# FoX key tiles in groups of two, first loads in two parts, and the causal mask as a GpSimd selection

## The chip, the cores and the metric

One core of a Trainium2 chip runs the whole program. The metric is the time of one execution on the device in microseconds (us), the median of several runs. The engines are TensorE (PE in the rows; PEld is its weight load), VectorE (DVE), ScalarE (ACT), GpSimd (POOL) and SyncE (SP), which issues nearly all transfers.

## The reference

A transformer block with two gated attention branches, in float32. For the change the FoX branch matters, causal attention with a forget gate:

```python
u = rmsnorm(h, g_pre);  q, k, v, z, f, gates = split(u @ w_in)
# FoX branch, 8 heads of 64, 1040 tokens (16 learned ones ahead of 1024)
logits = (q @ k.T) * 64**-0.5 + (c[t] - c[s])          # c = cumsum(log_sigmoid(f))
logits = where(s <= t, logits, -1e30)                  # the causal mask
y_fox = softmax(logits) @ v * silu(z_fox)
# SWA branch: a band of 128 tokens and the 16 learned ones, ALiBi, a sink in the softmax
m = sigmoid(g_swa) * (y_swa @ w_up_swa) + sigmoid(g_fox) * (y_fox @ w_up_fox)
out = h + rmsnorm(m @ w_out)
```

## The kernel before

The program has four stages, one behind the other on TensorE: RMSNorm, transposes and the plain projections; products for the other projections (query, gate, z), which end at 495 us; **attention**, 505 to 678 us; up-projection, merge and output. This case is about attention.

**FoX** runs over 4 pairs of heads (j), 2 halves of the queries (q, 512 columns each) and the key tiles of 128 (i: 5 for the first half, 9 for the second): 14 **units** a pair, 56 in all, numbered u. The function `key_tile` gives a unit's width, 512 columns, or 512, 400, 272, 144 and 16 where the diagonal cuts it; ten of fourteen units are cut by the diagonal and masked. For each unit TensorE does the step **tile** (key times query into PSUM, two float32r matmuls for each head, L1964 and L1965, and for a masked unit a bfloat16 matmul more, L1970, that adds -1e30 over up to 128 columns). ScalarE takes the exponential into the ring `p_fox` (L1352). The step **values** then multiplies it by V (L1984, four matmul records of 64 output rows), and GpSimd and VectorE add the exponentials up in `acc` (L1194, L1199 and L1749). When a half is complete, **den** sums `acc` over the keys on TensorE (L1994), ScalarE copies it to `den_row` (L1378), VectorE takes four reciprocals (**rec**, L1755) and multiplies (**fin**, L1762 and L1765).

**SWA** is spread between the units as 32 **items**: **score** on TensorE (L1944, L1945), maximum on VectorE (L1703 to L1711), exponential on ScalarE (L1364), reciprocal (`rec`, L1721) on VectorE and **norm** on GpSimd (L1175), transposes **trans** on TensorE (L2003), copied to `p_t` by ScalarE (even items) or VectorE (odd ones, L1727), **pv_swa** on TensorE (L2017) and the product with z into `y` on VectorE (L1734). There is one PSUM bank for pv_swa's result, so it waits for the y of the item before (`swa_y`).

`attention_steps` writes one list of steps. Every engine walks this list and issues its own part of each step, in that order and no other; semaphores hold the data together. An engine that waits in one step holds up all its later steps. In the list of before, unit u's tile is followed by a norm and a score, the values of unit u-1, an exponential, a den or rec, one pv_swa and one trans. The queries, keys and values of pair 0 are loaded by SyncE during the last couple of products, and behind them the values of SWA (`v_a`, `v_b`), for which the first score waits (`swa_loaded`).

Of the kernel before, what the change touches and what calls it, by code (L numbers as in the profile page):

```python
# [60 lines left out]
PT_RING = 6  # L61
PSWA_RING = 2
PROB_RING = 3
# [159 lines left out]
def attention_steps():  # L223
# [3 lines left out]
    def score(i):  # L227
        return item("score", i)
# [10 lines left out]
    spread = len(units) - 8  # L239
    next_item, unnormed, normed, untransposed, unvalued = 0, None, None, None, None  # L240
    closing = []
    for u, (j, q, i) in enumerate(units):
        first, last = i == 0, i == 4 * q + 4
        x = u % per
        steps.append(dict(kind="tile", j=j, q=q, i=i, u=u, first=first, last=last))
        if j + 1 < PAIRS:
            for turn, what in ((1, "load_queries"), (2, "load_z"), (3, "load_keys"), (5, "load_values")):
                if x == turn:
                    steps.append(dict(kind=what, j=j + 1, u=u))
        if (j, x) in ((0, 7), (0, 9)):  # L250
            steps.append(dict(kind="load_up", d=(x - 7) // 2, u=u))
        untransposed, normed = normed, unnormed
        if unnormed is not None:
            steps.append(item("norm", unnormed))
            unnormed = None
        slot = next_item < ITEMS and (u + 1) * ITEMS // spread > u * ITEMS // spread
        if slot:
            steps.append(score(next_item))
        if u:
            pj, pq, pi = units[u - 1]  # L260
            steps.append(dict(kind="values", j=pj, q=pq, i=pi, u=u - 1, first=pi == 0, last=pi == 4 * pq + 4))
        if slot:
            steps.append(item("exp", next_item))
            unnormed = next_item
            next_item += 1
        if closing and closing[0][0] <= u:
            steps += closing.pop(0)[1]
        if unvalued is not None:
            steps.append(item("pv_swa", unvalued))
            unvalued = None  # L270
        if untransposed is not None:
            steps.append(trans(untransposed))
            unvalued = untransposed
        if last:
            closing.append((u + 2, [dict(kind="den", j=j, q=q)]))
            closing.append((u + 3, [dict(kind="rec", j=j, q=q, c=c) for c in range(2)]))
            closing.append((u + 4, [dict(kind="rec", j=j, q=q, c=c) for c in (2, 3)] + [dict(kind="fin", j=j, q=q)]))
        if j == PAIRS - 1:
            turn = {1: 0, 3: 1, 5: 2, 7: PAIRS + 2, 9: PAIRS - 1, 10: PAIRS, 11: PAIRS + 1}
            if x in turn:  # L280
                steps.append(dict(kind="split_y", s=turn[x], c0=0, c1=2))
            if x == 12:
                steps.append(dict(kind="split_y", s=2 * PAIRS - 1, c0=0, c1=1))
            if x == 4:
                steps.append(dict(kind="split_up", d=0))
            if x == 8:
                steps.append(dict(kind="split_up", d=1))
    j, q, i = units[-1]
    steps.append(dict(kind="values", j=j, q=q, i=i, u=len(units) - 1, first=False, last=True))
    for _, extra in closing:  # L290
        steps += extra
    steps.append(dict(kind="split_y", s=2 * PAIRS - 1, c0=1, c1=2))
    assert next_item == ITEMS and unvalued is None and unnormed is None and untransposed is None and normed is None

    uses, count, splits = [], {"dve": 0, "act": 0}, 0
    for st in steps:
# [1815 lines left out]
```

## Time and profile before

| | us |
|---|---|
| median of 3 runs (lowest, highest) | 869.65 (867.27, 871.06) |
| the profiled execution's own time | 866.6 |
| its span | 864.8 |
| attention, first FoX matmul to first matmul of the up-projection | 505 to 678 |
| GpSimd busy from 505 to 678 | 103.8 |
| VectorE busy from 505 to 678 | 117.8 |

The span is the profiled execution from its first to its last instruction. In a row of a timeline the first number is the start in the span, the second the length, then engine, line, operation, output and inputs; in brackets stands the idle time before it and what ended that. A matmul's length is modelled and overlaps the next one's; the distance between two starts is what it takes.

### The profile page before, as it was taken

What the parts mean: (1) busy time and instruction counts of PE and PEld (TensorE: products, weight loads), DVE (VectorE), ACT (ScalarE), POOL (GpSimd) and SP (SyncE); (2) the same over time, 40 slices, a digit from 0 to 9 for tenths busy, and PEclk for the clock granted to TensorE, in tenths of its full rate; (3) what the DMA queues carried; (4) which work ended last, traced back from release to release, by engine and by line L of the source; (5) the groups of instructions that cost most, each with busy time, mean ns of one, the idle gap of its engine ahead of it and who ended that gap; (6) DMA issues with size and microseconds to landing.
All of it is one profiled execution on the core that took longest, in us unless ns stands there. A gap on an engine that the chain in (4) does not pass through costs nothing.

```text
span 864.8 us, 12858 instructions
## 1 busy us (share of the span) xinstructions
PE 809.0 (94%) x4514; PEld 651.2 (75%) x4514; DVE 500.1 (58%) x1050; ACT 314.6 (36%) x637; POOL 348.1 (40%) x284
## 2 busy tenths in 40 slices
PE   3999989999999999999999959998988799999996
PEld 3999989887878878878878746656654578878885
DVE  7934886357677686565564627676777434442112
ACT  6431241333333323333333236565667022232111
POOL 3412322444445444434444025655557244412221
PEclk9999999999999999999999979999999799999999
DMA  9331424569964626636635799946500645533221
GB/s 285 106 116 51 124 68 129 124 171 261 242 176 145 171 86 185 172 98 181 158 113 130 185 233 247 256 124 172 124 1 2 212 131 147 143 127 125 97 91 73
DMA packets 120879, 124.99 MB, mean 145 GB/s; under 512 B 29824, under 2 KB 91344, under 8 KB 120816
## 3 DMA queue, kind: packets, MB, share of 16 engines
q1 hardware_dynamic: 119376, 119.92, 50.9%
q10 hardware_dynamic: 1440, 4.26, 1.3%
q8 instruction: 36, 0.59, 0.3%
q14 instruction: 27, 0.22, 0.1%
HBM read 90.93 MB, written 34.92 MB: 146 GB/s over the span
## 4 chain that ended last, share of the span: by engine, by line
PE 76%; DVE 9%; issue 4%; SPq 3%; DMA 3%; POOL 2%; ACT 2%; DVEq 0%; ACTq 0%; POOLq 0%
PE PS L1827 18%; PE PS L1828 18%; PE PS L1829 18%; PE PS L2063 3%; PE PS L2065 3%; PE PS L2064 3%; PE PS L1924 2%; PE PS L1984 2%; DVE t_val L1579 2%; PE PS L1964 1%; SPq L871 1%; PE PS L1965 1%; PE PS L2003 1%; DMA QBs<-q_dram 1%; POOL acc L1199 1%
## 5 line engine op out<-in xcount | busy, mean ns | idle before, releaser
L1130 POOL TENSOR_TENSOR ops<-s_sum,ops 128x512 fp32r<-128x512 f32 x64 | 87.4, 1376 | 114.1 <-ACT ops L1228 114.1
L1827 PE MATMUL PS<-t_hi,ops 128*128 128x512 f32 x256 | 101.1, 395 | 0.0
L1828 PE MATMUL PS<-t_lo,ops 128*128 128x512 f32 x256 | 99.8, 390 | 0.0
L1829 PE MATMUL PS<-t_hi,ops 128*128 128x512 f32 x256 | 99.8, 390 | 0.0
L1130 POOL TENSOR_TENSOR ops<-raw,ops 128x512 fp32r<-128x512 f32 x48 | 65.0, 1354 | 70.0 <-ACT ops L1228 69.9
L1199 POOL TENSOR_TENSOR acc<-acc,p_fox 128x400 f32<-128x400 f32 (+5 forms) x76 | 61.5, 830 | 2.5 <-ACT p_fox L1352 0.9
L1151 POOL TENSOR_TENSOR w_plain<-raw,w_plain 128x1024 fp32r<-128x1024 f32 x10 | 28.0, 2801 | 85.0 <-ACT w_plain L1257 85.0
L1658 DVE TENSOR_TENSOR z_tmp<-u,PS 128x512 f32<-128x512 f32 x48 | 33.0, 687 | 48.9 <-PE PS L1829 28.1
L1352 ACT ACTIVATE p_fox<-PS,neg_c_col 128x512 f32<-128x512 f32 (+5 forms) x112 | 54.1, 532 | 17.2 <-PE PS L1970 14.4
L1228 ACT ACTIVATE ops<-s_sum 128x512 fp32r<-128x512 f32 x64 | 39.6, 624 | 54.9 <-DVE s_sum L1460 41.1
L1829 PEld LDWEIGHTS PS<-t_hi,ops 128*128 128x128 f32 x256 | 48.1, 188 | 10.6
L1827 PEld LDWEIGHTS PS<-t_hi,ops 128*128 128x128 f32 x256 | 48.3, 188 | 9.3
L1828 PEld LDWEIGHTS PS<-t_lo,ops 128*128 128x128 f32 x256 | 48.1, 188 | 8.9
L1964 PE MATMUL PS<-QA,KA 128*128 128x512 f32 (+5 forms) x112 | 42.9, 391 | 12.6 <-DMA KB<-k_dram 9.8
L1329 ACT ACTIVATE stage_b<-z_tmp,half_bg 128x512 f32<-128x512 f32 x32 | 23.2, 724 | 85.4 <-DVE z_tmp L1658 85.4
L1827 PE MATMUL PS<-y_hi,up_hi 128*128 128x512 f32 x128 | 51.0, 398 | 2.4 <-POOL up_lo L1136 1.4
L1175 POOL TENSOR_TENSOR probs<-probs,rec 128x416 f32<-128x416 f32 x32 | 29.6, 924 | 53.5 <-DVE rec L1721 53.5
L1827 PE MATMUL PS<-uA_hi,ops 128*128 128x512 f32 x128 | 50.9, 397 | 0.0
L1828 PE MATMUL PS<-uA_lo,ops 128*128 128x512 f32 x128 | 50.8, 397 | 0.0
L1828 PE MATMUL PS<-y_lo,up_hi 128*128 128x512 f32 x128 | 50.8, 397 | 0.0
L1829 PE MATMUL PS<-y_hi,up_lo 128*128 128x512 f32 x128 | 50.7, 396 | 0.0
L1829 PE MATMUL PS<-uA_hi,ops 128*128 128x512 f32 x128 | 50.3, 393 | 0.0
(203 smaller groups left out, 2192.1 us busy)
## 6 DMA issues: line engine op xcount, KB each, us to landing
raw<-in_w_in_dram SPq DMA_DIRECT2D x34, 512.0 KB, 5.2
q_dram<-stage_b SPq DMA_DIRECT2D x32, 256.0 KB, 3.0
g_dram<-stage_b SPq DMA_DIRECT2D x32, 256.0 KB, 2.0
tanh_g<-g_dram SPq DMA_DIRECT2D x16, 512.0 KB, 3.9
max_k<-k_dram SPq DMA_DIRECT2D x16, 260.0 KB, 5.3
max_c<-neg_c_dram SPq DMA_DIRECT2D x8, 520.0 KB, 6.0
KA<-k_dram SPq DMA_DIRECT2D x8, 520.0 KB
x_all<-in_x_dram SPq DMA_DIRECT2D x8, 512.0 KB, 8.1
```

Source lines behind the costliest of these rows:

```text
L1130: nc.gpsimd.tensor_tensor(ops[:, i % OPS, 1], op_source(p, name), ops[:, i % OPS, 0].bitcast(F32), ALU.subtract).then_inc(op_ready, 1)
L1151: nc.gpsimd.tensor_tensor(w_plain[:, t, 1], raw[:, s], w_plain[:, t, 0].bitcast(F32), ALU.subtract).then_inc(w_ready, 1)
L1175: nc.gpsimd.tensor_tensor(probs[:, b, :, 0:W_SWA], probs[:, b, :, 0:W_SWA], scale, ALU.mult).then_inc(swa_normed, 1)
L1199: nc.gpsimd.tensor_tensor(dst, other, tile, ALU.add).then_inc(acc_done["pool"], 1)
L1228: nc.scalar.activation(ops[:, i % OPS, 0], op_source(p, name), ACT.Copy).then_inc(op_hi_ready, 1)
L1352: nc.scalar.activation(p_fox[0:keys, n % PT_RING, 0:w], PS[0:keys, S_BANKS[n % S_RING], 0:w], ACT.Exp, bias=neg_c_col[0:keys, i, 2 * j + h ...
L1658: nc.vector.tensor_tensor(src, partial, product(p, "S1" if name == "S3" else name), ALU.add).then_inc(folded, 1)
L1827: pe.matmul(dst, hi_w, hi, start=first, stop=False)
L1828: pe.matmul(dst, hi_w, lo, start=False, stop=False)
L1829: return pe.matmul(dst, lo_w, hi, start=False, stop=last)
L1964: pe.matmul(dst, KA[n][:, h, kk], QA[n][:, h, tok], start=True, stop=False)
L2063: pe.matmul(dst, m_hi[:, k, tok], hi, start=k == 0, stop=False)
```

## The change

Four edits. (1) The list of steps goes by **groups** of two units, numbered g from 0 to 28: both tiles, the norms of the group before, one or two scores (a group with g divisible by 3 with rest 2 has two, up to g = 23), both values of the group before, exponentials, den with the first two reciprocals or the last two with fin, then all pv_swa of items scored two groups ago and all trans of items scored one group ago. (2) The causal mask leaves TensorE. GpSimd writes zeros over the masked part of the exponentials, two instructions for each of the 40 masked units, in the step values ahead of the additions, and the values matmul waits for them (`fox_masked`). (3) The first tiles of pair 0 wait for a first part of the loads alone (5 of 9 key tiles, half of the queries, 5 value tiles); the second parts are issued ahead of `v_a` and `v_b`, twelve transfers more in that place, and are waited for at unit 5. (4) `p_fox` has 8 buffers for 6, the ring `probs` 4 for 3.

```diff
-PT_RING = 6
+PT_RING = 8
-PROB_RING = 3
+PROB_RING = 4
@@ attention_steps: the list of steps, one group of two units at a time
-    spread = len(units) - 8
-    for u, (j, q, i) in enumerate(units):
-        steps.append(dict(kind="tile", j=j, q=q, i=i, u=u, first=first, last=last))
...
+    groups = len(units) // 2
+    spread = groups - 4
+    for g in range(groups + 1):
+        now = range(2 * g, 2 * g + 2) if g < groups else ()
+        for u in now:
+            steps.append(dict(kind="tile", j=j, q=q, i=i, u=u, first=i == 0, last=i == 4 * q + 4))
...
+        for n in scored:
+            steps.append(item("norm", n))
+        turned, scored = scored, []
+        if g < spread:
+            scored = list(range(g * ITEMS // spread, (g + 1) * ITEMS // spread))
+        for n in scored:
+            steps.append(score(n))
+        for u in range(2 * g - 2, 2 * g) if g else ():
+            j, q, i = units[u]
+            steps.append(dict(kind="values", j=j, q=q, i=i, u=u, first=i == 0, last=i == 4 * q + 4))
+        for n in scored:
+            steps.append(item("exp", n))
+        due = [x for x in closing if x[0] <= g]
+        closing = [x for x in closing if x[0] > g]
+        for _, extra in due:
+            steps += extra
+        for n in transposed:
+            steps.append(item("pv_swa", n))
+        for n in turned:
+            steps.append(trans(n))
+        transposed = turned
+        for u in now:
+            if i == 4 * q + 4 and g < groups - 1:
+                closing.append((g + 2, [den, rec 0, rec 1]))
+                closing.append((g + 3, [rec 2, rec 3, fin]))
...
@@ SyncE, in the last couple of the products
-                        load_values(sp, 0)
+                        load_values(sp, 0, fox_first, 0, 5)
-                        load_queries_fox(sp, 0)
+                        load_queries_fox(sp, 0, fox_first, 0, 4)
-                        load_keys_fox(sp, 0)
+                        load_keys_fox(sp, 0, fox_first, 0, 5 * P)
+                        load_keys_fox(sp, 0, fox_loaded[0], 5 * P, LENGTH)
+                        load_queries_fox(sp, 0, fox_loaded[0], 4, NQ)
+                        load_values(sp, 0, fox_loaded[0], 5, NK)
                         sp.dma_start(v_a[0:A_ROWS, 0, :], vd[0, 0:A_ROWS]).then_inc(swa_loaded, 16)
@@ GpSimd, at the step "values"
+                    for h in range(2):
+                        n = 2 * u + h
+                        if n in mask_of:
+                            tile = p_fox[n % PT_RING][0:keys, 0:masked]
+                            pool.wait_ge(fox_exp, n + 1)
+                            nc.gpsimd.affine_select(tile, tile, [[1, masked]], ALU.is_ge, 0.0, base=shift,
+                                                    channel_multiplier=-1).then_inc(fox_masked, 1)
@@ TensorE, at the step "tile"
-                    if i == 0 and q == 0:
+                    if (j, q, i) == (0, 0, 0):
+                        pe.wait_ge(fox_first, 16 * FIRST_LOADS)
+                        pe.wait_ge(halves_cleared, 3)
+                    elif i == 0 and q == (0 if j else 1):
                         pe.wait_ge(fox_loaded[j], 16 * FOX_LOADS)
-                    if masked:
-                        for h in range(2):
-                            pe.matmul(PS[0:keys, S_BANKS[(2 * u + h) % S_RING], 0:masked], causal[:, 0:keys],
-                                      ident_b[:, shift:shift + masked], start=False, stop=True).then_inc(tile_done, 1)
@@ TensorE, at the step "values"
                         pe.wait_ge(fox_exp, x + 1)
+                        if x in mask_of:
+                            pe.wait_ge(fox_masked, mask_of[x])
```

In the diff "den", "rec" and "fin" in the closing lists are written short. The order that comes out of it, first for **VectorE** around the den of pair 0's second half (group 8; `den_row` is rec of FoX, `rec<-den` is the reciprocal for a norm of SWA). Before:

```order
L1755 RECIPROCAL den_row<-den_row 128x128 x2
L1734 SCALAR_TENSOR_TENSOR y<-PS,y 128x128
L1727 COPY p_t<-PS 128x512
L1721 RECIPROCAL rec<-den 128x2
L1703 TENSOR_SCALAR far_alibi<-const 128x16
```

and with the change:

```order
L1786 RECIPROCAL den_row<-den_row 128x128 x2
L1763 SCALAR_TENSOR_TENSOR y<-PS,y 128x128
L1756 COPY p_t<-PS 128x512
L1750 RECIPROCAL rec<-den 128x2 x2
L1732 TENSOR_SCALAR far_alibi<-const 128x16
```

The order of kinds is the same; behind the two den reciprocals now stand two norm reciprocals, and the den itself stands in the same group's steps instead of one unit earlier.

**GpSimd** right behind that place, at group 9, whose values are those of units 16 and 17 (272 and 144 columns). Before:

```order
L1175 TENSOR_TENSOR probs<-probs,rec 128x2x208
L1199 TENSOR_TENSOR acc<-acc,p_fox 128x272 x2
L1175 TENSOR_TENSOR probs<-probs,rec 128x2x208
L1199 TENSOR_TENSOR acc<-acc,p_fox 128x144 x2
```

with the change:

```order
L1195 TENSOR_TENSOR probs<-probs,rec 128x2x208 x2
L1209 AFFINE_SELECT p_fox<-p_fox 128x128 x2
L1228 TENSOR_TENSOR acc<-acc,p_fox 128x272 x2
L1209 AFFINE_SELECT p_fox<-p_fox 128x128 x2
L1228 TENSOR_TENSOR acc<-acc,p_fox 128x144 x2
```

The selections stand behind two norms, and the second unit's behind the first unit's additions.

**TensorE** at units 7 and 8. Before, from the tile of unit 8 to one pv_swa:

```order
L1964 MATMUL PS<-QA,KA 128x512
L1965 MATMUL PS<-QB,KB 128x512
L1964 MATMUL PS<-QA,KA 128x512
L1965 MATMUL PS<-QB,KB 128x512
L1944 MATMUL PS<-kk_s,QAs 128x208
L1945 MATMUL PS<-kk_s,QBs 128x208
L1944 MATMUL PS<-kk_s,QAs 128x208
L1945 MATMUL PS<-kk_s,QBs 128x208
L1984 MATMUL PS<-p_fox,VF 64x512 x2
L2017 MATMUL PS<-p_t,v_a 64x128 x2
L2017 MATMUL PS<-p_t,v_b 64x128 x2
```

with the change, in group 4, behind the tiles of units 8 and 9 and a score:

```order
L2015 MATMUL PS<-p_fox,VF 64x512 x4
L2025 MATMUL PS<-acc,ones 64x512 x2
L2048 MATMUL PS<-p_t,v_a 64x128 x2
L2048 MATMUL PS<-p_t,v_b 64x128 x2
L2048 MATMUL PS<-p_t,v_a 64x128 x2
L2048 MATMUL PS<-p_t,v_b 64x128 x2
L2034 MATMUL PS<-ident,probs 80x128 x2
```

The values of two units (6 and 7) stand together, a den has come into the same group, and two pv_swa stand back to back.

## Rows read from the trace of the kernel before

**Rows 1.** Page, part 1: busy us, share of the span and instructions of each engine.
```profile
PE 809.0 (94%) x4514; PEld 651.2 (75%) x4514; DVE 500.1 (58%) x1050; ACT 314.6 (36%) x637; POOL 348.1 (40%) x284
```

**Rows 2.** Busy time in stretches of attention: PE, PEld, DVE, ACT, POOL, clock, DMA.
```profile
505.00:678.00 173.00, 154.68 (x1072) 98.25 (x1072) 117.75 (x339) 104.50 (x274) 103.81 (x122) 0.93 0.57 139
502.00:504.00 2.00, 0.00 (x0) 0.00 (x0) 0.00 (x0) 0.00 (x0) 0.00 (x0) 0.50 1.05 197
...
545.00:600.00 55.00, 52.21 (x386) 34.66 (x384) 37.43 (x120) 33.94 (x96) 32.18 (x42) 0.94 0.68 168
630.00:655.00 25.00, 20.54 (x132) 12.72 (x131) 16.87 (x45) 15.71 (x39) 15.69 (x19) 0.86 0.00 1
```

**Rows 3.** Waits of PE, 500 to 680: total, times, longest.
```profile
PE PS L1964 <- DMA KB<-k_dram: 9.8, 1, 9.8
PE PS L2017 <- DVE p_t L1727: 4.8, 3, 2.1
PE PS L1994 <- POOL acc L1199: 4.3, 2, 3.5
PE PS L1944 <- DVE neg_max L1711: 3.5, 2, 3.1
PE PS L1964 <- ACT p_fox L1352: 2.8, 5, 1.2
```

**Rows 4.** Timeline of PE in pair 1.
```profile
566.61 0.40 PE L1965 MATMUL PS<-QB,KB 128*128 128x512 f32 x1
566.94 1.08 PE L1984 MATMUL PS<-p_fox,VF 128*64 128x512 f32 x4
567.95 0.63 PE L2003 MATMUL PS<-ident,probs 128*80 128x128 f32 x4
...
569.11 0.39 PE L1965 MATMUL PS<-QB,KB 128*128 128x512 f32 x1
569.34 0.26 PE L1944 MATMUL PS<-kk_s,QAs 128*128 128x208 f32 x1
...
569.86 1.08 PE L1984 MATMUL PS<-p_fox,VF 128*64 128x512 f32 x4
570.77 0.39 PE L2017 MATMUL PS<-p_t,v_a 80*64 80x128 f32 x4
...
572.47 0.40 PE L1965 MATMUL PS<-QB,KB 128*128 128x512 f32 x1
...
572.80 0.34 PE L1944 MATMUL PS<-kk_s,QAs 128*128 128x208 f32 x1
...
573.41 1.08 PE L1984 MATMUL PS<-p_fox,VF 128*64 128x512 f32 x4
```

**Rows 5.** Groups by line and shape, 494 to 679: busy us, mean ns.
```profile
L1175 POOL TENSOR_TENSOR probs<-probs,rec 128x416 f32<-128x416 f32 x32 | 29.6, 924 | 53.5 <-DVE rec L1721 53.5
...
L1199 POOL TENSOR_TENSOR acc<-acc,p_fox 128x272 f32<-128x272 f32 x16 | 13.3, 852 | 0.0
...
L1199 POOL TENSOR_TENSOR acc<-acc,p_fox 128x144 f32<-128x144 f32 x16 | 8.0, 517 | 0.0
...
L1199 POOL TENSOR_TENSOR acc<-acc,p_fox 16x16 f32<-16x16 f32 x8 | 1.6, 211 | 0.0
```

**Rows 6.** Timeline of VectorE behind a den.
```profile
526.99 1.76 DVE L1755 RECIPROCAL den_row<-den_row 128x128 f32<-128x128 f32 x2
...
528.81 0.68 DVE L1727 COPY p_t<-PS 128x512 f32<-128x512 f32 x1
```

**Rows 7.** Timeline of SyncE's queue: last transfer before the first score.
```profile
494.92 0.62 SPq L1061 DMA_DIRECT2D v_b<-v_dram  x1
```

**Rows 8.** Transfers issued 478 to 520: KB each, median us to landing.
```profile
v_b<-v_dram SPq DMA_DIRECT2D x1, 512.0 KB, 13.1
```

**Rows 9.** Timeline of POOL at the end of attention.
```profile
663.01 5.37 POOL L1199 TENSOR_TENSOR acc<-acc,p_fox 128x512 f32<-128x512 f32 x3
669.07 5.98 POOL L1199 TENSOR_TENSOR acc<-acc,p_fox 128x400 f32<-128x400 f32 x7 [0.69 <-DVE acc L1749]
```

More of the change, by code:

```diff
@@ L238, in attention_steps @@
     per = len(units) // PAIRS
-    spread = len(units) - 8
-    next_item, unnormed, normed, untransposed, unvalued = 0, None, None, None, None
+    groups = len(units) // 2
+    spread = groups - 4
+    scored, transposed = [], []
     closing = []
-    for u, (j, q, i) in enumerate(units):
-        first, last = i == 0, i == 4 * q + 4
-        x = u % per
-        steps.append(dict(kind="tile", j=j, q=q, i=i, u=u, first=first, last=last))
[L246 to L287, printed above, removed]
@@ L288, in attention_steps @@
     j, q, i = units[-1]
-    steps.append(dict(kind="values", j=j, q=q, i=i, u=len(units) - 1, first=False, last=True))
-    for _, extra in closing:
-        steps += extra
+    steps += [dict(kind="den", j=j, q=q)] + [dict(kind="rec", j=j, q=q, c=c) for c in range(4)]
+    steps.append(dict(kind="fin", j=j, q=q))
     steps.append(dict(kind="split_y", s=2 * PAIRS - 1, c0=1, c1=2))
-    assert next_item == ITEMS and unvalued is None and unnormed is None and untransposed is None and normed is None
+    assert not closing and not scored and not transposed
@@ L442, in build @@
         VF[1] = sb("VF1", [P, NK, P], on=ph2)
-        p_fox = sb("p_fox", [P, PT_RING, BANK], on=ph2)
+        p_fox = [sb(f"p_fox{n}", [P, BANK], on=ph2) for n in range(6)]
         sb("gap", [P, 64], on=ph2)
@@ L843, in natural, with load_queries_fox @@
             return PS[:, 2 * (n % 4):2 * (n % 4) + 2, :].rearrange("p a b -> p (a b)")
-        def load_queries_fox(queue, j):
-            n, done = j % 2, fox_loaded[j]
-            q_hi, q_lo = (qd[PAIRS + j, x] for x in range(2))
+        def load_queries_fox(queue, j, done, t0, t1):
+            n, cols = j % 2, slice(P * t0, P * t1)
+            q_hi, q_lo = (qd[PAIRS + j, x][:, cols] for x in range(2))
             for half in (Q0, Q1):
-                queue.dma_start(QA[n][half].bitcast(F32),
+                queue.dma_start(QA[n][half, :, cols].bitcast(F32),
@@ L858, in load_keys_fox @@
-        def load_keys_fox(queue, j):
-            n, done = j % 2, fox_loaded[j]
-            k_hi, k_lo = (kd[1 + j, x] for x in range(2))
+                queue.dma_start(QB[n][row:row + 1, h, cols].bitcast(F32),
+                                max_dram[2 * j + h, t0:t1].rearrange("(o t) q -> o (t q)", o=1)).then_inc(done, 16)
+        def load_keys_fox(queue, j, done, c0, c1):
+            n, cols = j % 2, slice(c0, c1)
+            k_hi, k_lo = (kd[1 + j, x][:, cols] for x in range(2))
             for half, src in ((Q0, k_hi), (Q1, k_lo)):
-                queue.dma_start(KA[n][half].bitcast(F32),
+                queue.dma_start(KA[n][half, :, cols].bitcast(F32),
@@ L1189, in _ @@
                             continue
+                        if n in mask_of:
+                            pool.wait_ge(fox_masked, mask_of[n])
                         dst = acc[0:keys, f % 2, h, c0:c0 + w]
-                        tile = p_fox[0:keys, n % PT_RING, 0:w]
+                        tile = p_fox[n % PT_RING][0:keys, 0:w]
                         pool.wait_ge(fox_exp, n + 1)
```

77 lines of the change are left out of this document (56 added, 21 removed).

## The prediction

> **What bounds the kernel now.** The page's busy shares come first: TensorE is busy for 94% of the span, all others for 58% or less [rows 1]. Busy matmuls are modelled, so what counts is where TensorE waits, and the change touches attention alone. The stretches show 154.7 us of matmuls in the 173 us from 505 to 678, with VectorE at 117.8 and GpSimd at 103.8, at a mean clock of 0.93 [rows 2]. Behind this stands the table of TensorE's waits: 9.8 us for pair 0's keys, 4.8 for `p_t` from VectorE, 3.5 for a score's bank from VectorE, 2.8 for exponentials, and 4.3 for `acc` from GpSimd, of which 3.5 is one wait at the end [rows 3]. So TensorE bounds attention with little slack, and where it waits, VectorE or GpSimd is behind.
>
> **The change part by part. Matmuls of the mask.** 40 pairs go. With a mask the score starts 0.33 us after the last tile matmul (572.47 to 572.80), without 0.23 (569.11 to 569.34); and a score behind a mask takes 0.61 us to the values (572.80 to 573.41) against 0.52 (569.34 to 569.86) [rows 4]. That is 0.19 us for a mask ahead of a score (24 of them by the order) and 0.10 for the others (16): 4.6 + 1.6 = 6.2 us less.
>
> **Fewer changes of kind.** A values matmul behind a tile starts after 0.33 us (566.61 to 566.94), a matmul of the tile's own kind after 0.23; four values matmuls take 0.91 us to a pv_swa (569.86 to 570.77), which has the same 64 rows, and 1.01 to a trans (566.94 to 567.95) [rows 4]. So each change between the kinds costs 0.10 us. Counted in the order there are 141 in attention before and 77 now: 64 x 0.10 = 6.4 us less.
>
> **Waits that go.** If the new list were only denser, TensorE's waits in the middle would be other ones: I take out all of 4.8 + 3.5 + 2.8 + 0.8 = 11.9 us [rows 3], and the time at the lower clock, 6% of 55 us and 14% of 25 us [rows 2], 3.3 + 3.5 = 6.8 us. Together with the matmuls that is 31.3 us less. These are the credits.
>
> **The price of a selection.** The trace has no such instruction. Its nearest rows on GpSimd: 0.21 us for a sum of 16 x 16, 0.52 for a two-input sum of 144 columns [rows 5]. A selection over up to 128 columns with one input lies between; I take 0.30 us, 0.6 for a unit's two, 24 us in all on an engine that has 103.8 busy of 173 [rows 2]. That leaves room for the sum of work but not for the place: GpSimd does it behind the norms, ahead of which TensorE now waits.
> On GpSimd's elementwise work the Trainium skill ("GPSIMD Engine Reference", Elementwise side-by-side cycle accounting) gives about 2 cycles an element for a compare and select that is not unrolled and 2.6 for two inputs. An estimate from that page is 128 x 2.03 / 1.2 GHz = 0.22 us for a selection, and the row of 0.52 us for 144 columns is above its two-input figure (0.31), by a fixed part; with 0.22 the waits below would shrink by some 2 us.
>
> **The new chain of waits.** In before, GpSimd's norm is needed by a trans alone, and TensorE waited little for it. Now values wait for a selection, which waits behind the norms, which wait for VectorE's reciprocal, which in VectorE's order stands behind the den reciprocals, y and `p_t`. Two places show the size.
> *Group 9*, 0 being TensorE's start of group 8. Tiles of 272 and 144 columns, two scores, values of 512 and 400, den: matmuls until 4.6. ScalarE copies `den_row` until 5.3. VectorE then needs 1.8 us to `p_t` and 0.6 for that [rows 6]: 7.8. Only now come the two reciprocals and on GpSimd two norms of 0.88 [rows 5], until 9.6, and the first selection, 9.9. TensorE began group 9 at 5.6 and wanted it at 7.5: 2.4 us of waiting. The second unit's selection stands behind two sums of 272 columns, 0.73 each when they overlap (1.45 for two, [rows 5] gives 0.85 singly), and comes at 12.0, 1.5 us after TensorE is ready. Group 9 loses 3.9 us; groups 16 and 23, with one norm, 3.0 each.
> *Group 12* lies behind the den of the first half: the same chain, and two norms and a sum of 512 columns ahead of unit 23's selection: 3.1 us. Groups 5 and 19 have one norm, 2.3 each; group 26 has none left.
> *Groups 6, 13, 20* follow a group in which VectorE had rec, rec and fin behind a late sum; their norm starts some 2.7 us after TensorE wants the selection behind it, and two selections are waited for: 4.6 each, 5.4 in group 6 with two norms.
> Sum: 9.9 + 7.7 + 14.6 = 32.2 us.
>
> **Two pv_swa in one group** (8 groups). The second waits for the y of the first, which takes 0.2 us and a semaphore each way; I take 0.5 us: 4.0. In three of them (4, 22, 25) VectorE does two den reciprocals of 0.88 first [rows 6]: 1.6 more each, 4.8. Sum 8.8.
>
> **The end.** The last exponential sums run on GpSimd without a gap for 11.4 us [rows 9] and then release the den (the wait of 3.5 us [rows 3]). Ten selections come into this stretch: 3.0 us, and 1 us for a split that ScalarE now issues behind a den: 4.0.
>
> **The first loads.** They buy nothing. With half of the queries, three eighths of the keys and four ninths of the values no longer ahead (about 1.5 MB less at some 200 GB/s [rows 2]) TensorE starts pair 0 some 7 us earlier, does two tiles (2 us), and then the first score waits for `v_b`, as before. That transfer was issued at 494.92 and landed 13.1 us later, at 508.0 [rows 7, 8], with the DMA engines at 1.05 of their time [rows 2]: the bytes ahead of it are the same, and twelve more transfers, 0.6 us of issue each as the row of `v_b` has it [rows 7], put it at 502.6 on the queue. So it lands at 508 at the earliest, up to 510. Before, the score began at 508.9. And TensorE, idle again until then, starts at the lower level of its clock (granted 0.50 of 2.4 GHz in that stretch [rows 2]) with the whole list ahead instead of two tiles: 2.0 us more. From both sides: 1 us less to 4 us more.
> The Trainium skill speaks against this part ("DMA: Bandwidth & Descriptors", Rules for kernel authors): it advises few transfers of 1 MiB or more. By the trace the queue is full in any case; by the page the smaller pieces would also move fewer bytes a microsecond, which would put `v_b` later still, no earlier.
>
> **Sum.** 32.2 + 8.8 + 4.0 + 2.0 = 47.0 us more, 31.3 less: 15.7 more. Against the profiled execution's own 866.6 that gives 882.3; that execution lies 3.05 us below the median of 869.65, so the same difference on the median gives 885.4. I say 884.
>
> **The rivals.**
> *Faster, the list is dense and the chain is hidden* (0.29). VectorE and GpSimd had 32% and 40% of attention free [rows 2]. If VectorE reaches the norm's reciprocal two microseconds earlier than I reckon (the den's group starts late enough, or ScalarE's copy comes earlier), then the 32.2 us shrink to some 8, and the waits for pv_swa stay: 866.6 - 31.3 + 8 + 8.8 + 6 = 858, on the median 861; with the pv_swa waits at 0.5 us, 856. It decides from half of the mask waits on: below 16 us the change gains. For it speaks that TensorE waited for a norm hardly at all before; against it that VectorE's order puts four things ahead.
> *No change* (0.13): the mask waits come out at 13 to 20 us, 866 to 874.
> *Slower by much, GpSimd becomes the bound* (0.16). At 0.52 us a selection, the upper bound, GpSimd has 103.8 + 42 = 146 us to do in attention, in order, and idles wherever VectorE is late; each wait above grows by 0.4 to 0.9 us and the end by 2.2: 12 to 20 us more, 895 to 905.
> *My forecast* (0.42): 876 to 893.
> That the mask would not leave TensorE is excluded by the order.
>
> **How the numbers follow.** A measurement of this kernel tells 0.5% (4.3 us) from no change. Slower: 0.42 + 0.16 = 0.58; the same 0.13; faster 0.29. Since both signs hold much of the chance, the range must reach into the faster case: 854 leaves out about 0.12 below, 904 about 0.06 above. The likeliest case alone has 876 to 893.
>
> **What would show it.** Right: among TensorE's waits a new group, values (L2015) for GpSimd's selection (L1209), 20 to 40 us in some 15 times, the longest just behind a den; GpSimd idle for VectorE's `rec`; pv_swa waiting for `y`; the first score waiting 6 to 8 us for `v_b` with two tiles ahead of it; attention's end 12 to 20 us later. No L1970, and 64 steps of 0.1 us fewer, so TensorE's own busy time in attention down by about 10 us. Wrong: the selections come ahead of need, their waits sum to less than 16 us, or a selection takes over 0.4 us; the first score starts before 507.

## The result: 6.6% slower, against a forecast of 1.7%

| | us |
|---|---|
| changed kernel, median of 4 runs (lowest, highest) | 927.57 (926.54, 928.58) |
| kernel before, 4 runs beside it | 870.36 (867.27, 872.48) |
| ratio, 95% interval | 1.066 (1.0625 to 1.0696) |
| span of the profiled execution, after and before | 926.2 and 864.8 |
| first matmul of the up-projection, after and before | 739.7 and 678.1 |

The 61.4 us by which the spans differ lie in attention: the products end at 495 us in both, and the up-projection starts 61.6 us later. (The medians differ by 57.2 us; the profiled execution of the kernel before, 866.6 us, was 3.8 below the median beside it. What follows compares the two profiled executions.) The stretch from 495 to that matmul, first of the kernel before and then of the changed one (length, then busy time of PE, PEld, DVE, ACT and POOL, the granted clock, the DMA share and GB/s):

```profile
495.00:678.00 183.00, 154.85 (x1073) 98.35 (x1072) 118.44 (x341) 105.94 (x276) 103.81 (x122) 0.92 0.59 143
```

```profile
495.00:739.70 244.70, 174.60 (x995) 119.39 (x993) 120.74 (x341) 108.22 (x276) 119.09 (x202) 0.82 0.46 107
```

By the page of the profile TensorE is busy for 90% of the span ([rows 1] has 94):

```profile
PE 830.4 (90%) x4434; PEld 674.1 (73%) x4434; DVE 502.0 (54%) x1050; ACT 316.8 (34%) x637; POOL 363.5 (39%) x364
```

In the stretch TensorE has 78 records fewer and is busy for 19.8 us more; the clock fell from 0.92 to 0.82. It is idle for 42 us more (70.1 for 28.2). So work and waits both grew, and the forecast had only the waits: it expected less work.

The waits of TensorE in the changed kernel from 495 to 745, the counterpart of [rows 3]:

```profile
PE PS L2015 <- POOL p_fox L1209: 36.0, 22, 5.2
PE PS L2048 <- DVE y L1763: 14.2, 8, 3.7
PE PS L1998 <- ACT p_fox L1381: 8.3, 12, 2.0
PE PS L1975 <- DMA v_b<-v_dram: 6.9, 1, 6.9
PE PS L1998 <- DMA KB<-k_dram: 2.7, 1, 2.7
```

The first is the new wait, values for the selection; the second is a group's second pv_swa, waiting for y of the first. How the longest of the first kind arises is seen in three timelines of group 6. VectorE:

```profile
546.51 1.76 DVE L1786 RECIPROCAL den_row<-den_row 128x128 f32<-128x128 f32 x2
548.30 0.69 DVE L1793 SCALAR_TENSOR_TENSOR den_row<-den_row,y 128x512 f32<-128x512 f32 x1
549.03 0.69 DVE L1796 TENSOR_TENSOR y<-PS,den_row 128x512 f32<-128x512 f32 x1
549.64 0.28 DVE L1763 SCALAR_TENSOR_TENSOR y<-PS,y 128x128 f32<-128x128 f32 x1
549.84 0.68 DVE L1756 COPY p_t<-PS 128x512 f32<-128x512 f32 x1
550.43 0.22 DVE L1750 RECIPROCAL rec<-den 128x2 f32<-128x2 f32 x2
```

GpSimd, in brackets its idle time and what ended it:

```profile
550.67 1.71 POOL L1195 TENSOR_TENSOR probs<-probs,rec 128x416 f32<-128x416 f32 x2 [7.31 <-DVE rec L1750]
552.33 0.54 POOL L1209 TENSOR_SCALAR_AFFINE_SELECT p_fox<-p_fox 128x128 f32<-128x128 f32 x2
552.84 2.01 POOL L1228 TENSOR_TENSOR acc<-acc,p_fox 128x400 f32<-128x400 f32 x2
554.80 0.54 POOL L1209 TENSOR_SCALAR_AFFINE_SELECT p_fox<-p_fox 128x128 f32<-128x128 f32 x2
```

and TensorE:

```profile
552.77 1.81 PE L2015 MATMUL PS<-p_fox,VF 128*64 128x400 f32 x4 [5.23 <-POOL p_fox L1209]
555.24 1.39 PE L2015 MATMUL PS<-p_fox,VF 128*64 128x272 f32 x4 [0.66 <-POOL p_fox L1209]
```

The two reciprocals that the norms need take 0.22 us, and stand behind 3.9 us of closing work. ScalarE had finished the exponentials of these units at 542.6 (four from 540.53 on, 2.06 us), and GpSimd has been idle for 7.3 us, so it could have made the selections long before; in its order they stand behind the norms. So an engine with half of its time free holds up the one that is the bound.

What such a wait does afterwards is seen in group 9. Stretches of the changed kernel: the wait, what follows it, and the next 7 us.

```profile
573.20:576.80 3.60, 0.18 (x3) 0.06 (x1) 3.56 (x13) 1.55 (x5) 2.13 (x4) 0.98 1.05 316
576.80:583.00 6.20, 5.20 (x25) 3.90 (x26) 2.44 (x5) 0.60 (x1) 3.35 (x7) 0.50 1.03 220
583.00:590.00 7.00, 6.45 (x46) 4.50 (x44) 2.30 (x11) 4.47 (x10) 2.55 (x7) 0.96 0.74 157
```

After 3.4 us of idle time TensorE works for 6.2 us at 0.50, which is the lower of its two levels, 1.2 GHz.

### The profile page after: what moved, and what is told of

Its sections match the earlier page's. It is cut to its first block, busy times and chain, and to the rows that moved or that the text cites. A ratio compares the mean times of both kernels' runs of the same rounds, so it can differ in the third digit from the quotient of the medians.

```text
span 926.2 us, 12871 instructions
## 1 busy us (share of the span) xinstructions
PE 830.4 (90%) x4434; PEld 674.1 (73%) x4434; DVE 502.0 (54%) x1050; ACT 316.8 (34%) x637; POOL 363.5 (39%) x364
## 4 chain that ended last, share of the span: by engine, by line
PE 63%; issue 11%; POOL 6%; DVE 6%; ACT 2%; DVEq 0%; ACTq 0%; POOLq 0%; DMA 0%
PE PS L1858 14%; PE PS L1859 14%; PE PS L1860 14%; PE PS L2094 3%; PE PS L2095 3%; PE PS L2096 3%; POOL acc L1228 2%; PE PS L1955 2%; PE PS L2015 2%; POOL probs L1195 1%; PE PS L2048 1%; PE PS L2034 1%; POOL p_fox L1209 1%; PE PS L1998 1%; PE PS L1999 1%
## 5 line engine op out<-in xcount | busy, mean ns | idle before, releaser
L2015 PE MATMUL PS<-p_fox,VF 128*64 128x512 f32 (+5 forms) x224 | 56.0, 552 | 36.1 <-POOL p_fox L1209 36.0
L1195 POOL TENSOR_TENSOR probs<-probs,rec 128x416 f32<-128x416 f32 x32 | 28.2, 893 | 128.3 <-DVE rec L1750 124.5
L2015 PEld LDWEIGHTS PS<-p_fox,VF 128*64 128x64 f32 (+1 forms) x224 | 18.9, 154 | 57.1 <-issue 49.9
L1687 DVE TENSOR_TENSOR z_tmp<-u,PS 128x512 f32<-128x512 f32 x48 | 32.9, 686 | 48.9 <-PE PS L1860 28.2
L1228 POOL TENSOR_TENSOR acc<-acc,p_fox 128x400 f32<-128x400 f32 (+5 forms) x76 | 55.5, 747 | 0.6
L1998 PE MATMUL PS<-QA,KA 128*128 128x512 f32 (+5 forms) x112 | 45.3, 411 | 11.2 <-ACT p_fox L1381 8.3
L1858 PE MATMUL PS<-uA_hi,ops 128*128 128x512 f32 x128 | 50.8, 397 | 0.0
```

Of the source, the lines that this page charges most:

```text
L1195: nc.gpsimd.tensor_tensor(probs[:, b, :, 0:W_SWA], probs[:, b, :, 0:W_SWA], scale, ALU.mult).then_inc(swa_normed, 1)
L1228: nc.gpsimd.tensor_tensor(dst, other, tile, ALU.add).then_inc(acc_done["pool"], 1)
L1687: nc.vector.tensor_tensor(src, partial, product(p, "S1" if name == "S3" else name), ALU.add).then_inc(folded, 1)
L1858: pe.matmul(dst, hi_w, hi, start=first, stop=False)
L1998: pe.matmul(dst, KA[n][:, h, kk], QA[n][:, h, tok], start=True, stop=False)
L2015: ins = pe.matmul(PS[h * HEAD:(h + 1) * HEAD, Y_BANKS[f % 2], c0:c0 + w], VF[j % 2][0:keys, i, h * HEAD:(h + 1) * HEAD], p_fox[x % PT_RING ...
```

## The experiments

Fifteen kernels, each read against the kernel before in its own runs. Beside the times stand numbers of the profiled execution from 495 us on: the selection and y columns are TensorE's waits for each; "ends" is the first matmul of the up-projection.

| kernel | median us | ratio (95%) | ends | PE busy | clock | selection | y |
|---|---|---|---|---|---|---|---|
| changed | 927.57 | 1.066 (1.0625 to 1.0696) | 739.7 | 174.6 | 0.82 | 36.0 | 14.2 |
| loads_one_part | 928.22 | 1.0657 (1.0626 to 1.0688) | 739.7 | 177.9 | 0.80 | 32.0 | 14.2 |
| fill_waits | 914.76 | 1.0493 (1.0451 to 1.0535) | 725.4 | 183.8 | 0.94 | 20.4 | 5.6 |
| mask_only | 914.53 | 1.0494 (1.0469 to 1.0518) | 726.8 | 171.4 | 0.83 | 47.4 | 0 |
| rec_early | 904.47 | 1.0376 (1.0352 to 1.0399) | 715.1 | 162.2 | 0.85 | 13.5 | 24.2 |
| select_first | 897.65 | 1.0302 (1.0271 to 1.0333) | 709.8 | 158.8 | 0.87 | 9.0 | 18.7 |
| groups_pe_mask | 893.43 | 1.0253 (1.0228 to 1.0279) | 704.5 | 161.8 | 0.88 | none | 19.6 |
| select_first_den_last | 889.93 | 1.0208 (1.0172 to 1.0245) | 700.5 | 153.8 | 0.92 | 7.4 | 9.1 |
| mask_first | 889.72 | 1.0205 (1.0161 to 1.025) | 701.5 | 161.3 | 0.87 | 27.0 | 0 |
| all_three | 888.96 | 1.0195 (1.0157 to 1.0232) | 699.6 | 153.8 | 0.90 | 7.4 | 13.2 |
| groups_pe_mask_den_last | 888.57 | 1.0175 (1.0123 to 1.0227) | 700.2 | 162.5 | 0.89 | none | 7.7 |
| groups_pe_mask_all | 886.02 | 1.0157 (1.012 to 1.0195) | 697.8 | 161.5 | 0.90 | none | 7.5 |
| all_four | 884.44 | 1.0143 (1.0095 to 1.0192) | 696.2 | 154.1 | 0.91 | 6.6 | 9.7 |
| late_values | 874.67 | 1.0039 (1.0015 to 1.0063) | 689.2 | 155.5 | 0.90 | 7.4 | 0 |
| rings_only | 872.12 | 1.0004 (0.9984 to 1.0023) | 684.0 | 157.2 | 0.90 | none | 0.6 |
| no_mask_before | 868.26 | 0.9958 (0.9943 to 0.9973) | 680.1 | 151.3 | 0.91 | none | 0.7 |

### One part undone, or one alone

**groups_pe_mask**, the mask back on TensorE:

```diff
-                        pe.matmul(dst, KB[n][:, h, kk], QB[n][:, h, tok], start=False, stop=True
-                                  ).then_inc(tile_done, 1)
+                        ins = pe.matmul(dst, KB[n][:, h, kk], QB[n][:, h, tok], start=False, stop=not masked)
...
+                            pe.matmul(PS[0:keys, S_BANKS[(2 * u + h) % S_RING], 0:masked], causal[:, 0:keys],
+                                      ident_b[:, shift:shift + masked], start=False, stop=True).then_inc(tile_done, 1)
```

Expected: 

> The changed kernel with the causal mask back on TensorE as before (all matmuls of the mask, no selection); groups, rings and the first loads in two parts stay. Chain theory (values wait for a selection that stands behind the norms; these 36 us of waits also take TensorE to its lower clock): the waits of values for GpSimd go, waits for a norm at the transposes come back for at most 8 us, mean clock in attention above 0.90, 880 to 892 us. Rival, the groups themselves are at fault (two pv_swa, scores, den and tiles in bundles, each engine in lockstep): the waits only move to the transposes and pv_swa, clock stays below 0.87, 905 to 925 us.

893.4: the selection accounts for 34 of the 57 us, and the groups alone cost 22 (first loads and rings included, which cost nothing that can be told, see below). Neither theory had it whole: the time is 1.4 us above the chain theory's range and the clock 0.88. The waits here are for y (19.6 us), for exponentials (11.1 in 18 places, against 2.8 in [rows 3]) and for norms (2.6).

**mask_only**, the other half: the selection in the kernel before, in its step values.

Expected: 

> The kernel before with the mask as a GpSimd selection alone, in the step values behind the norm; no groups, no split loads, rings as before. Chain theory: one norm for each unit stands ahead of each selection and VectorE's reciprocal ahead of that, 10 to 25 us of waits for the selection appear and the clock falls to 0.88 or so: 875 to 895 us. Rival, the groups are at fault: the selection alone is hidden, 4 to 7 us of mask matmuls are saved, 862 to 867 us.

914.5, beyond the range of both. The table of waits and, below it, one place on GpSimd:

```profile
PE PS L1998 <- POOL p_fox L1195: 47.4, 27, 4.3
PE PS L1981 <- DMA KB<-k_dram: 9.7, 1, 9.7
PE PS L2031 <- DVE p_t L1742: 1.6, 1, 1.6
```

```profile
631.93 0.88 POOL L1181 TENSOR_TENSOR probs<-probs,rec 128x416 f32<-128x416 f32 x1 [4.28 <-DVE rec L1736]
632.76 0.54 POOL L1195 TENSOR_SCALAR_AFFINE_SELECT p_fox<-p_fox 128x128 f32<-128x128 f32 x2
```

The same chain as in group 6, without any group: reciprocal, norm, selection, values. By itself the mask costs 4.9%, the groups 2.5%; together 6.6%. That the two don't add up would fit one wait that serves both units of a group (27 waits in `mask_only`, 22 in the changed kernel); no run shows it by itself.

**loads_one_part**, pair 0's loads as before:

```diff
-                        load_keys_fox(sp, 0, fox_first, 0, 5 * P)
-                        load_keys_fox(sp, 0, fox_loaded[0], 5 * P, LENGTH)
-                        load_queries_fox(sp, 0, fox_loaded[0], 4, NQ)
-                        load_values(sp, 0, fox_loaded[0], 5, NK)
+                        load_keys_fox(sp, 0, fox_loaded[0], 0, LENGTH)
```

Expected: 

> The changed kernel with pair 0's first loads in one part as before. My reckoning of the split (2 us lost, bounds 1 gained to 4 lost): 922 to 928 us, and the mean clock of attention stays at 0.82. Rival, the early start and the second wait for v_b are a main cause: below 915 us.

928.2, the ratio within 0.0003 of the changed kernel's, each known to some 0.003: the split does nothing that can be told. Its rows in the changed kernel are those foreseen, two tiles early and then the wait for `v_b`:

```profile
497.98 0.59 PE L1998 MATMUL PS<-QA,KA 128*128 128x512 f32 x1 [2.67 <-DMA KB<-k_dram]
...
508.10 0.54 PE L1975 MATMUL PS<-kk_s,QAs 128*128 128x208 f32 x1 [6.91 <-DMA v_b<-v_dram]
```

**rings_only**, the kernel before with 8 buffers for `p_fox` and 4 for `probs`. Expected: 

> The kernel before with the larger rings alone (8 buffers of exponentials for 6, 4 of probs for 3); mask on TensorE, no groups, no split loads. If buffers were never what was waited for: 869 to 872 us. If they take away a part of the waits for exponentials and accumulations: 863 to 868 us.

1.0004 (0.9984 to 1.0023): no effect that can be told.

**no_mask_before**, the kernel before with no mask at all. Expected: 

> The kernel before with the causal mask left out altogether (no mask matmul and no selection; its FoX branch attends to later tokens too). It sizes what taking the mask off TensorE can bring at most. My term was 6.2 us for the matmuls (0.19 and 0.10 us each): 862 to 866 us. Rival, VectorE and GpSimd pace the attention stage and the matmuls lie in their shadow: 868 to 872 us.

868.3, 0.42% faster (0.27 to 0.57%), 3.6 us. The stretch from 495 shows the same 3.6 us less of busy time (151.27 for 154.85), though in these two profiled executions the stretch itself isn't shorter (185.1 us for 183.0):

```profile
495.00:680.09 185.09, 151.27 (x994) 97.07 (x993) 118.39 (x341) 105.86 (x276) 103.78 (x122) 0.91 0.61 141
```

So in the order of before 40 pairs of mask matmuls cost 0.09 us each, not the 0.155 of my term, and no way of masking elsewhere could have won more than these 3.6 us (2.4 to 5.0). Two things limit the reading of busy times. `rings_only` has the matmuls of the kernel before and is busy for 157.2 us in its profiled execution, 2.3 more, so single executions agree to 2 or 3 us. And in the order by groups the mask matmuls show more: `groups_pe_mask_all` is busy for 161.5 us, `all_four` without them for 154.1, at clocks of 0.90 and 0.91, while their times differ by only 1.6 us.

### The place of the selection

**select_first** puts a group's selections ahead of its norms:

```diff
@@ GpSimd
+                if kind == "tile" and st["u"] >= 2 and st["u"] % 2 == 0:
+                    select(st["u"] - 2)
+                    select(st["u"] - 1)
```

Expected: 

> The changed kernel with the selections of a group issued by GpSimd ahead of the group's norms instead of behind them; nothing else. Chain theory: the waits of values for the selection fall from 36 to below 12 us, the clock rises from 0.82 to 0.88 or more, 885 to 900 us. Rival, the groups are at fault: other waits (pv_swa for y, tiles for exponentials, transposes for norms) grow in their place, 912 to 925 us. Rival, GpSimd has too much to do: its order changes nothing, 920 to 930 us.

897.7: the waits for the selection fall from 36.0 to 9.0 us, and the time by 30. Not all of this is waits. TensorE's idle time in the stretch fell by 14 us in all, since others took the place of some: y rose to 18.7, exponentials to 11.1, so a part of the rival holds too. The other 16 us are useful work, the same matmuls, which went from 174.6 to 158.8 us at a clock of 0.87.

**rec_early** attacks the same chain from VectorE:

```diff
@@ VectorE
-                elif kind == "norm":
+                elif kind == "exp":
                     i, b = st["i"], st["i"] % PROB_RING
                     dve.wait_ge(swa_exp, 2 * (i + 1))
```

Expected: 

> The changed kernel with VectorE's reciprocal for a norm moved to the end of its own group's scores, ahead of the den reciprocals, y and p_t, instead of the start of the next group; GpSimd's order unchanged (selection behind the norm). Chain theory as in the prediction (the reciprocal at the end of VectorE's group holds up norm and selection): waits for the selection fall from 36 to below 20 us, 895 to 912 us. Rival, GpSimd's own order (norms of 0.88 us and sums ahead of the selection) holds it up: 920 to 930 us. Rival, VectorE now waits for ScalarE's exponentials and is late with the sums and y: 928 us or more.

904.5: 36.0 to 13.5 us, with GpSimd's order as it was. Both ends of the chain are thus shown. The second rival takes its share: at `rec` VectorE now waits for ScalarE's exponentials for 22.6 us (1.6 before), and the waits for y come to 24.2 us.

**mask_first** and **late_values** do it in the order of before, unit by unit; `late_values` also has the larger rings and the values one unit later:

```diff
-        if u:
-            pj, pq, pi = units[u - 1]
+        if u > 1:
+            pj, pq, pi = units[u - 2]
```

Expected of the first: 

> The kernel before with the mask as a GpSimd selection alone (no groups, no split loads), and this time each unit's selection stands in the step tile of the next unit, ahead of the norm. Chain theory (what costs is the place behind the norm and VectorE's reciprocal): the 47 us of waits that the same selection cost behind the norm fall below 12, clock in attention back above 0.90, 862 to 875 us. Rival, GpSimd has 24 us more to do in a strict order and the norms and sums come late instead: 885 to 905 us.

Expected of the second: 

> The order of the kernel before, unit by unit, with the larger rings and the mask as a GpSimd selection issued in the tile step of the next unit, and the values of a unit one unit later than before (two units behind its tile), so that the selection has a whole unit of slack. Chain theory (it is the slack between a selection and its values matmul that decides): hardly any wait for a selection, clock above 0.92, 861 to 870 us. Rival, GpSimd's 24 us more in strict order are too much whatever the slack: 878 to 890 us.

`mask_first` gives 889.7, which lies in the rival's range and not in the theory's. Its mechanism is neither of the two pure: 27.0 us of waits for the selection remain, and no norm is waited for. The selection now stands ahead of its own unit's norm, but still behind the norm and the sums of the step before, so the old chain goes on through them. GpSimd at one of these waits, which ends at 516.51 after 2.89 us:

```profile
513.27 0.88 POOL L1194 TENSOR_TENSOR probs<-probs,rec 128x416 f32<-128x416 f32 x1 [3.55 <-DVE rec L1744]
514.10 2.01 POOL L1222 TENSOR_TENSOR acc<-acc,p_fox 128x400 f32<-128x400 f32 x2
516.07 0.54 POOL L1183 TENSOR_SCALAR_AFFINE_SELECT p_fox<-p_fox 128x128 f32<-128x128 f32 x2
```

`late_values` gives 874.7, 4.7 us above the theory's range and 3 below the rival's. Its waits, in a profiled execution of 877.9 us (the ten lie between 871.8 and 879.3):

```profile
PE PS L1997 <- DMA KB<-k_dram: 9.7, 1, 9.7
PE PS L2014 <- POOL p_fox L1191: 7.4, 5, 4.1
PE PS L1977 <- DVE neg_max L1742: 6.6, 4, 2.2
PE PS L2047 <- DVE p_t L1758: 4.4, 3, 2.8
```

With the same 80 selections on GpSimd the loss shrinks from 4.9% to 0.4%. Slack between a selection and its values, not GpSimd's throughput, is what the mask lacks. What remains in `late_values` is no gain all the same: `no_mask_before`, which has the same matmuls in the order of before and no selections, is 6.4 us faster.

### What a wait costs afterwards

**fill_waits** leaves the changed kernel as it is and adds matmuls that nobody reads, in 13 places ahead of the values and in 4 groups ahead of the second pv_swa:

```diff
+            def fill(group, times):
+                x, n = min(4 * group + 1, 111), min(group // 7, 3) % 2
+                pe.wait_ge(fox_exp, x + 1)
+                for _ in range(times):
+                    pe.matmul(PS[:, S_BANKS[x % S_RING], :], KA[n][:, 0, 0:P], QA[n][:, 0, 0:BANK],
+                              start=True, stop=True)
...
+                if kind == "values" and st["u"] in FILL:
+                    fill(st["u"] // 2 + 1, FILL[st["u"]] * 3 // 4)
```

Expected: 

> The changed kernel with some 120 matmuls more that nothing reads (keys times queries of 512 columns into a free score bank, 0.23 us each at the upper level, some 28 us together), placed on TensorE ahead of the waits for the selection and for y that were longer than 1 us; they should fit into the waits. Clock theory (the waits also cost afterwards, since TensorE then works at 1.2 GHz for a while): with more matmuls the kernel gets faster, mean clock above 0.90, 897 to 915 us. Rival (the lower level costs nothing, since VectorE and GpSimd set the pace): the clock rises and the time stays or grows, 925 to 940 us.

914.8 against 927.6: with more work the kernel is 12.8 us faster. The stretch, and the group of added matmuls:

```profile
495.00:725.41 230.41, 183.84 (x1112) 126.24 (x1112) 119.88 (x340) 107.61 (x276) 119.67 (x202) 0.94 0.50 114
```

```profile
L1968 PE MATMUL PS<-QA,KA 128*128 128x512 f32 x119 | 31.5, 404 | 0.0
```

Group 9 again: the wait, what follows it, and the next 7 us.

```profile
573.20:576.00 2.80, 2.52 (x12) 1.72 (x10) 2.77 (x12) 1.60 (x6) 2.04 (x4) 1.00 1.06 248
576.00:580.30 4.30, 2.74 (x24) 2.04 (x25) 2.39 (x4) 0.15 (x2) 3.44 (x7) 1.00 1.03 220
580.30:587.00 6.70, 6.14 (x47) 4.40 (x46) 2.45 (x11) 4.53 (x11) 2.16 (x6) 1.00 1.04 210
```

and single steps of it, the eight transposes and the next tile, in the changed kernel and then with the filling:

```profile
580.89 1.93 PE L2034 MATMUL PS<-ident,probs 128*80 128x128 f32 x8
...
582.47 0.78 PE L1998 MATMUL PS<-QA,KA 128*128 128x512 f32 x1
```

```profile
573.21 2.50 PE L1968 MATMUL PS<-QA,KA 128*128 128x512 f32 x10
...
579.49 1.07 PE L2050 MATMUL PS<-ident,probs 128*80 128x128 f32 x8
580.32 0.48 PE L2014 MATMUL PS<-QA,KA 128*128 128x512 f32 x1
```

Both begin to wait at 573.2 and both get the selection at 576 to 577; the next group starts at 582.47 in one and at 580.32 in the other. Ten added matmuls take 2.5 us here, so the 119 take about 30 (31.5 by the row above), and the useful work comes to some 154 us, 20 less than in the changed kernel. Idle and filled time together are 76 us, 6 more than it idled; the whole gain is faster work, at 0.94 for 0.82. The rival, in which VectorE and GpSimd set the pace, had 925 to 940 us and is out. The kernel `select_first_den_last` comes to the same 153.8 us at 0.92 with no filling.

### What the groups cost by themselves

Five kernels put further orders right. **den_last** moves den, rec and fin behind pv_swa and the transposes; **all_three** adds rec_early to it; **all_four** puts the second pv_swa behind the transposes too; **groups_pe_mask_all** has all of these with the mask on TensorE. The order of steps in the last two, against the changed kernel:

```diff
-        due = [x for x in closing if x[0] <= g]
-        closing = [x for x in closing if x[0] > g]
-        for _, extra in due:
-            steps += extra
-        for n in transposed:
+        for n in transposed[0:1]:
             steps.append(item("pv_swa", n))
         for n in turned:
             steps.append(trans(n))
+        for n in transposed[1:]:
+            steps.append(item("pv_swa", n))
         transposed = turned
+        due = [x for x in closing if x[0] <= g]
+        closing = [x for x in closing if x[0] > g]
+        for _, extra in due:
+            steps += extra
```

Expected of select_first_den_last: 

> The changed kernel with the selections ahead of the norms on GpSimd, and den, rec and fin at the end of their group, behind pv_swa and the transposes, on every engine. Theory (the second pv_swa of a group waits for y, which on VectorE stands behind two reciprocals of 0.88 us and, elsewhere, behind a whole round of two engines): the waits for y fall from 18.7 to below 8 us, 873 to 886 us. Rival (the groups as such keep the engines in lockstep): the waits move to the tiles' exponentials and the transposes, 892 to 900 us.

Expected of groups_pe_mask_den_last: 

> Groups of two, first loads in two parts and the larger rings, but the mask as matmuls on TensorE, and den, rec and fin at the end of their group. Same theory as for the selection with that order: waits for y from 19.6 to below 8 us, 870 to 882 us. Rival, lockstep of the groups: 888 to 895 us.

Expected of all_three: 

> The changed kernel with three orders altered together: selections ahead of the norms on GpSimd, VectorE's norm reciprocal at the end of its own group's scores, and den, rec and fin behind pv_swa and the transposes. If the causes found are the whole loss beside the second pv_swa and the start: 876 to 884 us. If groups of two hold the engines in lockstep beyond these: 887 to 892 us, as with the first and third alone (889.9).

Expected of all_four: 

> As all_three, and where a group has two pv_swa the second stands behind the transposes, so that y of the first has time. If the round of y between two pv_swa (0.55 us at least in 8 groups) is a cost of its own: 4 to 8 us below all_three. If not: within 2 us of it.

Expected of groups_pe_mask_all: 

> Groups of two with the mask as matmuls on TensorE, den, rec and fin at the end of the group, VectorE's norm reciprocal early, the second pv_swa behind the transposes: what the groups cost with every order found to matter put right and no selection at all. If the groups in themselves are harmless: 868 to 876 us. If tiles in pairs cost (three score banks for four tiles, so that the second tile of a group waits for exponentials, 13 us in the run without the last two edits): 880 to 888 us.

They give 889.9, 888.6, 889.0, 884.4 and 886.0. By the ratios, den last is worth 0.9% with the selection and 0.8% without. The reciprocal on top of it is worth nothing that can be told. The second pv_swa behind the transposes gives 4.5 us, with intervals that overlap. All orders together leave 1.4 to 1.6%, with or without a selection, so this rest belongs to the groups. Its largest waits, in `groups_pe_mask_all`:

```profile
PE PS L1996 <- ACT p_fox L1379: 11.7, 17, 2.4
PE PS L2051 <- DVE y L1761: 7.5, 6, 2.9
PE PS L1973 <- DMA v_b<-v_dram: 6.1, 1, 6.1
PE PS L2028 <- POOL acc L1226: 5.5, 1, 5.5
```

Tiles waiting for exponentials are, by the order of steps, what pairs of tiles bring: four scores want three banks (`S_RING`), and 11.7 us stand against 2.8 in [rows 3]. No run shows it: a fourth bank could settle it, but all eight banks of PSUM are in use, and it wasn't tried. So how the rest divides stays open.

## Why the prediction was wrong

From 495 us on, the forecast had 35.1 us more of idle time (47.0 less the 11.9 of waits that go) and 19.4 less of work (6.2 + 6.4 + 6.8). Measured: 42 more idle and 19.8 more of work. **Waits were missed by 7 us, the work by 39.** So:

**The waits for the selection were right in kind and nearly in size, the size in part by luck.** 32.2 us were forecast for the selection in some 15 places, 36.0 came in 22. Group 6: 5.4 forecast, 5.23 + 0.66 measured; group 9: 3.9 and 3.42 + 1.00; group 12: 3.1 and 3.94; group 16: 3.0 and 2.9. Groups 13 and 20, 4.6 each in the forecast, had 3.2 and none; groups 5 and 23, 2.3 and 3.0, had none and 1.0. In their place group 24 waits for 3.54, and groups 27 and 28, at the end, for 1.8 and 2.9. The price of a selection, taken at 0.30 us and the disputed number beforehand, was no error: all 80 take 24.4 us on GpSimd, 0.305 each, and two of 128 columns mostly 0.54. The estimate of 0.22 was too low. GpSimd was busy for 119 of 245 us, which sets the rival in which it becomes the bound aside.

**Two pv_swa in one group** was mis-sized: 8.8 us forecast, 14.2 measured. Four of eight came out at 0.54 to 0.56 as taken. The other four waited 2.3 to 3.7. One of them, group 19 with 3.63, wasn't among the three that the forecast named: VectorE does the last two reciprocals of a den and `fin` there ahead of y, from 662.64 to 665.8. In the three named ones the reciprocals ahead of y were late themselves. In group 4 on VectorE:

```profile
536.27 1.76 DVE L1786 RECIPROCAL den_row<-den_row 128x128 f32<-128x128 f32 x2 [1.49 <-ACT den_row L1407]
537.95 0.23 DVE L1763 SCALAR_TENSOR_TENSOR y<-PS,y 128x128 f32<-128x128 f32 x1
```

and on ScalarE, whose copy of the den stands behind a tile's exponential, which waits for a buffer that VectorE's sum frees:

```profile
534.17 0.69 ACT L1381 ACTIVATE p_fox<-PS,neg_c_col 128x512 f32<-128x512 f32 x1 [1.28 <-DVE acc L1780]
...
535.66 0.58 ACT L1407 ACTIVATE den_row<-PS 128x512 f32<-128x512 f32 x1
```

**Waits that go** did not all go. Those for `p_t` and neg_max did, but tiles waited 8.3 us for exponentials where 2.8 had been: by the order of steps three score banks and four scores, which I had not reckoned with.

**The end** was forecast at 4.0 us on top of the den's wait of 3.5 [rows 3]. The den waits no more; the last values wait instead, 1.8 + 2.9 us, counted above with the selection.

**The clock had the wrong sign, and this is the step that failed.** The forecast took "the time at the lower clock" as something that goes, 6.8 us, in the same text that added 40 us of new waits. At 0.92, as before, the same matmuls take 153.8 us (`select_first_den_last`); at 0.82 they take 174.6. So 20.8 us are owed to the clock, and the 6.8 were not gained: 27.6 of the 39. `fill_waits` shows the cause apart from the waits. Read in steps of 0.25 us, TensorE was busy at the lower level for 70 us in the changed kernel, 24 in `select_first_den_last` and 19 in the kernel before; half of the differences, since that level is half of the upper one, is 23 and 25 us. So the clock's part is known to some 3 us. I had the evidence: [rows 2] show 0.86 in the stretch with the most waits and 0.94 elsewhere.
The Trainium skill says how to price it ("TensorE: Matmul & The Clock Gate", HAM oscillation — how this bites in real kernels): the loss is the time spent throttled times one half. By that rule a mean of 0.82 over 244.7 us is 88 us at the lower level, against 29 before, and an estimate of 30 us of loss. The runs show 20.8, less. Part of the throttled time is idle: of the 88 us TensorE is busy in 70, and of the 29 in 19, and by busy time alone the rule gives 25.

**The credits of matmuls** were too large: 12.6 us forecast, 1.1 measured at an equal mean clock (154.85 to 153.75; if the clock's part is put at 25 us, some 5). The mask's own part is 3.6 in the order of before, by the run without a mask. I had read 0.19 us off two starts of a timeline [rows 4], an interval in which other things differ too. What was left of it, 6.4 us for fewer changes of kind, did not show: without a mask in both, the order of before is busy for 151.3 us and the groups for 153.8. That makes 11.5 of the 39.

**The first loads** were right in their mechanism and cost nothing that can be told, where 2.0 us were forecast.

With the clock's 27.6 us put right the forecast of 884 would have been 912, already above the range's end of 904; with the credits too, 923. Each rival moved a wait by some 0.5 us or halved them; none asked what 50 us of waits would do to the work between them.

## What to carry to other kernels

Ask what stands ahead of a cheap step on the engine that it moves to: the same 80 selections cost 4.9% behind the norm, 2.1% ahead of it, and 0.4% with the values one unit later, and an engine's free half is no help in a strict order. New waits on TensorE are priced twice, once as idle time and once as the work after them at the lower clock; here 42 us of the one brought some 21 of the other, and a credit for "less low clock" must not stand beside a sum of new waits. Size the most that a change can win by leaving the step out altogether: it was 3.6 us here, in the order of before.

## What the runs showed of the hardware

Waits of 3.4, 3.9 and 5.2 us (groups 9, 12 and 6) were each followed by work at 1.2 GHz, for 6.2, 2.9 and 6.8 us; one of 2.0 us for exponentials, ended at 598.67, by work at 2.4. The length of a single wait doesn't decide it alone: four waits of 0.63, 0.61, 0.88 and 1.32 us, the last ended at 685.78, were followed by work at 0.50 from 686 to 689. The stretches behind the waits of 5.2, 3.9 and 2.0 us:

```profile
552.70:559.50 6.80, 6.07 (x25) 4.38 (x26) 0.42 (x2) 0.60 (x1) 4.07 (x7) 0.50 0.00 1
...
604.60:607.50 2.90, 2.90 (x12) 1.81 (x13) 2.70 (x3) 0.00 (x0) 1.30 (x2) 0.52 0.00 0
...
598.67:602.00 3.33, 1.97 (x10) 0.97 (x10) 3.33 (x12) 1.54 (x4) 1.17 (x2) 1.00 0.00 0
```

Useless matmuls in the waits bought back 12.8 us net, at the slow edge of what was expected of them (897 to 915 us). On GpSimd two selections in place, one behind the other, take 0.54 us for 128 columns each and 0.34 for 16, so more than half of the price doesn't hang on the columns. Some take longer: between 723 and 735 us in the changed kernel four pairs of 112 and 128 columns took 0.99 to 1.97 us, and why, no run shows.
